# A fused two-block transformer on one core: the head norm of the delta layer taken into the output projection, wider norm sums, modulation sums out of the first weight slab, and a mask and a weight part moved in each pair of dilated heads

## The reference

```python
def _gated_deltanet(qkv, gate, ...):
    ...
    q = (_l2norm(q) * (DN_HEAD_K ** -0.5))
    k = _l2norm(k)
    ...
    o = o * lax.rsqrt(jnp.mean(o * o, axis=-1, keepdims=True) + EPS) * g_out   # the head norm, 4 heads of 128
    o = o * jax.nn.silu(gate)

def first_block(x, mem, ...):
    ...
    mix = jnp.concatenate([attn_o, dn_o], axis=-1) @ w_out        # features 0-511 attention, 512-1023 delta layer
    x = x + _rms_norm(mix, g_mix_post)
    c = _memory_cross_attention(_rms_norm(x, g_cross_pre), _rms_norm(mem, g_mem), w_cq, w_ckv, w_co)
    x = x + _rms_norm(c, g_cross_post)
    f = _swiglu(_rms_norm(x, g_ffn_pre), w_gate_up, w_down)
    x = x + _rms_norm(f, g_ffn_post)

def second_block(x, c, ...):
    mod = (silu(c) @ w_ada + b_ada)                               # shift, scale, gate of each part
    h = h + 0.5 * gt * swiglu(modulate(rms_norm(h, norm_g), sh, sc), ffn_w_in, ffn_w_out)
    ...
def dilated_mixer(u, ...):
    # 3 groups: q, k = rope(rms_norm(.)), banded attention, softmax over the groups
```

## Time and profile before

| | |
|---|---|
| three runs, us | 3774.03, 3776.29, 3779.77 (median 3776.29) |
| profiled execution, us | 3775.3 |
| its span, us | 3773.5 |
| mean granted clock of PE | 0.976 |
| PE busy, share of the span | 3598.0 us, 95% |
| DVE busy | 1940.0 us, 51% |
| ACT busy | 1436.7 us, 38% |
| product matmuls L848, L853, L854 on x | 2936 each |

### The profile page before, as it was taken

The page is one execution under the profiler, slowest core; times in us unless marked ns, Lnnn a source line. Parts: engine busy times, 40 slices in busy tenths (PEclk is TensorE's granted clock), DMA queues, the critical chain, the costliest instruction groups (busy, mean ns, idle before and its releaser), DMA issues.

```text
span 3773.5 us, 49208 instructions
## 1 busy us (share of the span) xinstructions
PE 3598.0 (95%) x18880; PEld 2897.3 (77%) x18880; DVE 1940.0 (51%) x3906; ACT 1436.7 (38%) x2555; POOL 107.7 (3%) x183
## 2 busy tenths in 40 slices
PE   7989999999999999999999989999899998889999
PEld 6879976878887888766666668888788886678887
DVE  6767665565565545555555554334433345764333
ACT  3342132422232222555665643223322234863222
POOL 0000001011001000000000000000000000000000
PEclk9999999999998999999999989999899999999999
DMA  5200046145544554211111212222222220012222
GB/s 212 95 1 1 1 156 245 67 139 189 176 165 141 178 184 134 70 65 51 51 68 51 79 54 89 89 103 91 76 100 101 73 92 29 2 46 89 90 92 76
DMA packets 47156, 359.74 MB, mean 95 GB/s; under 512 B 5216, under 2 KB 5600, under 8 KB 28128
## 3 DMA queue, kind: packets, MB, share of 16 engines
q1 hardware_dynamic: 23472, 269.35, 19.6%
q0 software_dynamic: 23472, 87.50, 6.9%
HBM read 354.73 MB, written 2.10 MB: 95 GB/s over the span
## 4 chain that ended last, share of the span: by engine, by line
PE 84%; DVE 7%; issue 3%; ACT 3%; DVEq 1%; DMA 1%; ACTq 0%; PEld 0%; PEldq 0%; POOL 0%; SPq 0%; POOLq 0%
PE bank L848 22%; PE bank L854 22%; PE bank L853 21%; PE bank L1775 5%; PE bank L2093 1%; PE bank L2081 1%; PE bank L2591 1%; DVE w_lo_sb L1285 1%; PE bank L2558 1%; PE bank L989 1%; PE bank L2069 1%; PE bank L828 1%; PE bank L810 1%; PE bank L2580 1%; PE bank L2108 1%
## 5 line engine op out<-in xcount | busy, mean ns | idle before, releaser
L848 PE MATMUL bank<-x_hi_sb,w_hi_sb 128*128 128x512 f32 x2936 | 1177.4, 401 | 54.9 <-DVE w_lo_sb L1285 16.3
L854 PE MATMUL bank<-x_hi_sb,w_lo_sb 128*128 128x512 f32 x2936 | 1152.1, 392 | 0.0
L853 PE MATMUL bank<-x_lo_sb,w_hi_sb 128*128 128x512 f32 x2936 | 1151.3, 392 | 0.0
L848 PEld LDWEIGHTS bank<-x_hi_sb,w_hi_sb 128*128 128x128 f32 x2936 | 555.4, 189 | 226.1 <-issue 82.0
L1108 ACT ACTIVATE w_hi_sb<-slab_sb 128x1024 fp32r<-128x1024 f32 (+2 forms) x555 | 508.4, 937 | 511.0 <-PE bank L848 317.5
L1285 DVE TENSOR_TENSOR w_lo_sb<-slab_sb,w_hi_sb 128x1024 fp32r<-128x1024 f32 (+2 forms) x555 | 581.7, 1078 | 199.5 <-ACT w_hi_sb L1108 185.7
L854 PEld LDWEIGHTS bank<-x_hi_sb,w_lo_sb 128*128 128x128 f32 x2936 | 555.2, 189 | 120.1
L853 PEld LDWEIGHTS bank<-x_lo_sb,w_hi_sb 128*128 128x128 f32 x2936 | 556.4, 190 | 110.0 <-issue 0.5
L1451 DVE TENSOR_TENSOR hid_sb<-silu_gate_sb,bank 128x512 f32<-128x512 f32 x110 | 75.6, 687 | 600.3 <-PE bank L854 600.3
L848 PE MATMUL bank<-hid_hi_sb,w_hi_sb 128*128 128x512 f32 x880 | 342.8, 390 | 0.0
L854 PE MATMUL bank<-hid_hi_sb,w_lo_sb 128*128 128x512 f32 x880 | 342.6, 389 | 0.0
(11 more groups left out here) (368 smaller groups left out, 3696.5 us busy)
## 6 DMA issues: line engine op xcount, KB each, us to landing
slab_sb<-weights SPq DMA_DIRECT2D x79, 2048.0 KB, 7.9
keep_sb<-ada POOLq DMA_DIRECT2D x137, 512.0 KB, 4.5
slab_sb<-weights SPq DMA_DIRECT2D x44, 1536.0 KB, 6.5
slab_sb<-weights SPq DMA_DIRECT2D x20, 1280.0 KB, 6.0
tables_sb<-ada POOLq DMA_DIRECT2D x12, 512.0 KB, 6.0
work_sb<-ada POOLq DMA_DIRECT2D x11, 512.0 KB, 5.6
h_sb<-x SPq DMA_DIRECT2D x4, 512.0 KB, 7.6
out<-h_sb SPq DMA_DIRECT2D x8, 256.0 KB, 2.1
```

The lines of the kernel that those rows point to most:

```text
L848: mm = pe.matmul(out, w_hi[p][:, w], hi, start=first, stop=False)
L853: pe.matmul(out, w_hi[p][:, w], lo, start=False, stop=False)
L854: return pe.matmul(out, w_lo[p][:, w], hi, start=False, stop=last)
```

## The change

Six edits in one:

- Stage "delta_out" is gone. `pe_delta_out` sums the four heads' squares (32 columns of ones in place of one), runs 8 fillers, and begins the first slab of w_out with k-tiles 0 to 3 (attention, which needs no head norm) of its four output tiles, with the head norm's spreads after the first and second of them, two heads each, into the two banks of the scores ring; then k-tiles 4 to 7 of the four tiles. ACT squares head by head, DVE scales and gates each head between weight parts. `mem` is loaded after "delta", and the next modulation rows after the heads are done.
- The norm sums are 128 columns wide (`P`), and 42 (`WIDE`) where three sums share a bank. The count of matmuls stays.
- The window's 32 sums become 8 matmuls with 512 columns and weights 64 wide (`one_slots`, two per step into the two halves of a bank), a copy by ACT (`rows_summed`) and four transposes, and everything after them that `pe_delta_ahead` does comes one step earlier. The 12 decay sums become 3 with more columns.
- No modulation sum stands in a "first" step; "mid" and "last" get them.
- In each dilated pair the first two instructions of mask(1) go ahead of weigh(0), and `w_lo_part(7)` ahead of `rope(1, 0)` (on ACT `w_hi_part(7)` ahead of `swap_in(1, 0)`).
- 9 fillers stand ahead of `stage_end("ffn_down")`; `OUT_SEAT` 1 becomes 0 (which bank is used); a semaphore is gone.

```diff
-OUT_SEAT = 1
+OUT_SEAT = 0
+WIDE = 42
...
+        def sums_in(bank, n, wide):
+
+            return bank[:, n * NB * wide:(n + 1) * NB * wide].rearrange("p (b w) -> p b w", w=wide)
+
-        def pe_sums_of(e, n, tile):
+        def pe_sums_of(e, n, tile, stop=False):
 
             for b in range(NB):
-                at = n * NB + b
-                e.eng.matmul(e.S.bank[e.sums][:, at:at + 1], tile[:, b * P:(b + 1) * P], ones1, start=at == 0, stop=False)
+                mm = e.eng.matmul(sums_in(e.S.bank[e.sums], n, e.wide)[:, b, :], tile[:, b * P:(b + 1) * P],
+                                  K("ones")[:, 0:e.wide], start=n == b == 0, stop=stop and b == NB - 1)
+            return mm
 
         def pe_sums_open(e, cross=None, first=False):
 
             pe = e.eng
-            e.sums = e.give(e.S, e.sc)
+            e.sums, e.wide = e.give(e.S, e.sc), P if cross is None else WIDE
...
-            if i < 2:
-                if i == 0:
-                    e.norms = e.give(e.A, e.acc)
-                for j in DN_TILES[4 * i:4 * i + 4]:
...
-                    for b in range(NB):
-                        at = j * NB + b
-                        mm = pe.matmul(e.A.bank[e.norms][:, at:at + 1], sq[:, j, b * P:(b + 1) * P], ones1, start=True,
-                                       stop=True)
...
+            if i == 0:
+                s = e.give(e.A, e.acc)
+                for n in range(4):
+                    pe.wait_ge(squared, e.nth(squared))
+                    pe.wait_ge(queries_squared, n + 1)
+                    for x in range(2):
+                        mm = pe.matmul(e.A.bank[s][HALF * x:HALF * x + HALF, :], K("one_slots")[:, 3 - n:67 - n],
+                                       sq[:, 4 * x + n, :], start=n == 0, stop=n == 3)
+                mm.then_inc(e.A.full[s], 1)
+            if i == 1:
+                pe.wait_ge(rows_summed, 1)
+                t = e.give(tp, e.tp)
+                for b in range(NB):
+                    mm = pe.transpose(turn_bank[t][:, b * P:(b + 1) * P], sq[:, 0, b * P:(b + 1) * P], ident)
+                mm.then_inc(tp.full[t], 1)
...
             e.stage_end("delta")
-            pe_stay_busy(e, 10)
-            pe_cols(e, f_t, 4, NB, False, 1, 6)
-            for j in range(4):
-                pe_spread(e, NB, 1, j)
-            e.stage_end("delta_out")
...
+        def pe_delta_out(e):
...
+            pe_stay_busy(e, 8)
+            e.slab.next()
+            ps, seats = [], []
+            for t in range(PARTS):
+                ps.append(e.take(part, e.part))
+                seats.append(e.give(e.A, e.acc))
+                for kt in range(DH):
+                    if t == 0:
+                        pe.wait_ge(x_lo_ready, e.nth(x_lo_ready))
+                    pe_product(e, seats[t], ps[t], slice(kt * P, (kt + 1) * P), x_hi[:, kt, :], x_lo[:, kt, :], kt == 0, False)
+                if t == 0:
+                    pe.wait_ge(inverted, e.nth(inverted))
+                if t < 2:
+                    spread(2 * t)
+                    spread(2 * t + 1)
+            for t in range(PARTS):
+                for kt in range(DH, KT):
+                    if t == 0:
+                        pe.wait_ge(x_lo_ready, e.nth(x_lo_ready))
...
+            for j in range(DH):
+                s = e.take(e.S, e.sc)
+                e.link(dve.scalar_tensor_tensor(out=y[:, DH + j, :], in0=y[:, DH + j, :], scalar=V("g_dn_out"),
+                                                in1=e.S.bank[s][:, :], op0=ALU.mult, op1=ALU.mult), dve_step)
+                tt(y[:, DH + j, :], y[:, DH + j, :], b1_gate[:, j, :], ALU.mult).then_inc(scaled, 1)
+                dve.drain().then_inc(e.S.free[s], 1)
+                if j < 2:
+                    dve_w_lo(e, 2 + j, D)
+            dve.drain().then_inc(normed, 1)
+            for k in range(DH, KT):
+                low(k)
...
             out_tile(0)
+            mask(1, 0)
             weigh(0)
             out_tile(1)
-            mask(1)
+            mask(1, 1)
...
             mask(3)
+            w_lo_part(7)
             rope(1, 0)
-            w_lo_part(7)
...
             def modulations(half, at):
-                if at in ("first", "mid", "last"):
-                    dve_ada(e, 2 if at == "mid" else 3)
-                elif half == 0:
+                if at in ("mid", "last"):
+                    dve_ada(e, 3 - half)
+                elif at != "first" and half == 0:
                     dve_ada(e, 1)
...
-            if stage_over("delta_out"):
+            if stage_over("delta"):
                 eng.dma_start(mem_in, a["mem"]).then_inc(mem_loaded, 16)
+                eng.wait_ge(normed, KT + DH + 1)
                 load_ada(1)
```

More of the change, by code:

```diff
@@ L1020, in pe_sums_close @@
                 for b in range(NB):
-                    at = n * NB + b
-                    mm = pe.matmul(e.S.bank[e.sums][:, at:at + 1], tile[:, b * P:(b + 1) * P], ones1,
-                                   start=False, stop=at == len(tiles) * NB - 1)
+                    mm = pe.matmul(sums_in(e.S.bank[e.sums], n, e.wide)[:, b, :], tile[:, b * P:(b + 1) * P],
+                                   K("ones")[:, 0:e.wide], start=False, stop=n == len(tiles) - 1 and b == NB - 1)
             mm.then_inc(e.S.full[e.sums], 1)
@@ L1060, in act_root @@
             s = e.take(ring, seat)
-            act.activation(root[:, 0:cols], ring.bank[s][:, 0:cols], ACT.Sqrt, scale=scale,
+            sums = ring.bank[s][:, 0:cols * wide].rearrange("p (b w) -> p b w", w=wide)[:, :, 0]
+            act.activation(root[:, 0:cols], sums, ACT.Sqrt, scale=scale,
                            bias=small[:, 120:121]).then_inc(rooted, 1)
@@ L1713, in act_delta_ahead @@
             act = e.eng
-            if i == 2:
-                act_root(e, 32, 1.0)
+            if i == 0:
+                s = e.take(e.A, e.acc)
+                act.activation(sq[:, 0, :], e.A.bank[s][:, :], ACT.Copy).then_inc(rows_summed, 1)
+                act.drain().then_inc(e.A.free[s], 1)
+            if i == 1:
+                t = e.take(tp, e.tp)
+                act.activation(root[:, 0:32].rearrange("p (x n b) -> p b x n", x=2, n=4),
+                               turn_bank[t][:, :].rearrange("p (b x c) -> p b x c", b=NB, x=2)[:, :, :, 0:4], ACT.Sqrt,
+                               bias=small[:, 120:121]).then_inc(rooted, 1)
+                act.drain().then_inc(tp.free[t], 1)
                 act_table(e, ACT.Exp)
@@ L2369, in take_scores, with mask, roots, mask_first @@
                 return s
-            def mask(u):
+            def mask(u, half=None):
                 if not attending:
                     return
+                if half != 1:
+                    mask_first(u)
+                if half != 0:
+                    mask_others(u)
+            def roots(u):
+                return [[d_inv[old][:, 6 * u + 2 * g + hh:6 * u + 2 * g + hh + 1] for hh in range(2)] for g in range(3)]
+            def mask_first(u):
                 if u == 3:
@@ L2956, in out_tile @@
                 act_copy_square(e, k, f_t[:, k, :])
-            act_linear_parts(e, y, 1, out_tile, first=4, ahead=0)
+            for k in range(KT):
+                out_tile(k)
+                if k < PARTS:
+                    act_w_hi(e, k, D)
             e.stage_end("w_out")
@@ L3235, in out_tile @@
                     dve_ada(e, 2)
-            dve_linear_parts(e, y, 1, out_tile, first=4, ahead=0)
+            for k in range(KT):
+                out_tile(k)
+                if k < PARTS:
+                    dve_w_lo(e, k, D)
             e.stage_end("w_out")
@@ L3274, in later_modulations @@
             def later_modulations(half, at):
-                if at in ("first", "mid", "last"):
-                    dve_ada(e, 2)
-                elif half == 0 or at == 0:
+                if at in ("mid", "last"):
+                    dve_ada(e, 2 if at == "mid" else 3)
+                elif at != "first" and (half == 0 or at == 0):
                     dve_ada(e, 1)
```

111 lines of the change are left out of this document (68 added, 43 removed).

## The result

The changed kernel takes 3722.19 us (median of 4 runs, 3718.33 to 3724.34) against 3777.15 for the kernel before: a ratio of 0.9855, 95% interval 0.9839 to 0.987. 3725 was forecast. The profiled execution took 3722.46, its span 3720.7.

What follows compares the result with a forecast made beforehand. PE bounds the kernel (84% of the span), losing time standing still or at half clock. Gains 13.3 + 11.5 + 8.4 + 10 + 8 = 51.2 from 3775.3 give 3724, plus 1.0 for the median: 3725 us, range 3709 to 3746.

Steps and rivals of the forecast that it cites:

- A: Head norm in w_out: attention products start before the head norm, tile 3 done at 500.2; gain 13.3 us, from 9.5 to 15.
- D: Dilated pairs: PE's waits for w_lo (6.6 us) and mask (5.2 us) go; gain 10 us, from 4 to 12.
- 32 sums at 0.117 are 3.7, 16 fillers 1.9: Ahead of w_out's first product: sums and fillers from 469.1 us at 0.117 us each, so products start at 474.7.
- B: Norm sums: wider columns cost nothing and keep the clock at full where narrow sums ran at half; 11.5 us, 0 to 20.
- 6.7 and half of 9.9: Wide norm sums: 6.7 us from 1524.2 and later stretches; 9.9 us at 746 and 1131.7, halved for having only 42 columns.
- C: First steps of two FFNs: without modulation sums, waits shrink 3.1 and 1.9 us, half clock returns 1.7 each; 8.4, 5 to 9.
- I give 1.8 back: Dilated pairs: new waits on weigh and rope take back a quarter of a microsecond in each of seven pairs.
- E: Window stage: 16 instructions of 512 columns replace two groups of 32 sums, fewer decay sums; gain 8 us, from 4 to 11.
- The clock rival: Norm and window sums: clock falls regardless of width, wide sums gain 0, window part 4.8; 3740 us, chance 0.17.
- The dilated waits did not move: Rival, dilated stage: PE waits for weigh(0) or rope instead, gain there 0 to 2 us; 3733 to 3735, chance 0.10.
- w_out did not stall behind DVE: Rival, w_out: DVE's scalings run 6 us late, PE waits some 3 us ahead of k-tile 4; 3730 us, chance 0.08.
- wait for a modulation row: Rival, fourteen pairs taking three rows: POOL's refill takes about 18 us, PE waits in each; 3776 or more, chance 0.03.

## Why the prediction held, step by step

The time came 3 us below the forecast, inside the range. That it came so near is luck: A is below its low bound, D above its high one, and the two errors cancel.

- **A** (13.3, at least 9.5): 8.2. The mechanism of the overlap was right: attention half first, spreads between, the scalings beside the products, and mem hidden, with no wait where I feared one (the spread of head 3 or k-tile 4). The failed step is "32 sums at 0.117 are 3.7, 16 fillers 1.9": I took the full clock of before for granted, though the change removed the ten fillers that stood ahead of the sums, where PE then stood still 2.07 us. The half clock cost 5.0; fillers in that place gave back 3.5.
- **B** (11.5; its terms, 6.7 and half of 9.9, make 11.65): 9.8 in the profiled pair, 8.7 by medians and 8.3 by products on taking it back. It is a little oversized, and its reason held only in part. I wrote that the wide sums rest on the clock falling "during narrow ones", and counted the fillers as a cost to be hidden. Between the FFNs the fillers do the larger part: all of 4.2 in the changed kernel, and in the kernel before as much as the width alone, 3.5 and 3.6. Width works behind w_ckv: in all nine traces with wide sums the lead grows by 1.5 to 1.6 there, and in none with narrow ones. At the end of the second FFN it gives 0.8, in seven of the nine. The failed step is "the clock fell during narrow ones. This is what the wide sums rest on": 42-wide sums went at half too, for 10.2 us behind w_co. My half for 42 columns was the right caution for a wrong reason: behind w_co they gave nothing in the changed kernel and 4.6 in the run with wide sums alone.
- **C** (8.4): 8.0, both waits and both falls of the clock as stated; the ten pairs with three sums show no wait. That the clock falls behind the second, shorter wait is not sure: it did not when the sums were put back.
- **D** (10, at most 12): 18.3. The step that failed is "I give 1.8 back" and, under it, taking the idle time of the earlier trace rows as the price, over a window that ends ahead of the last round. Nothing was given back, and the two moves are worth 7.7 and 7.2 by products. A wait shown as 0.83 costs more, as PE's timeline in the kernel before shows (start, duration, idle before):

```profile
1640.50 0.40 PE L854 MATMUL bank<-x_hi_sb,w_lo_sb 128*128 128x512 f32 x1
1641.73 0.50 PE L848 MATMUL bank<-x_hi_sb,w_hi_sb 128*128 128x512 f32 x1 [0.83 <-DVE w_lo_sb L1285]
1642.07 0.39 PE L853 MATMUL bank<-x_lo_sb,w_hi_sb 128*128 128x512 f32 x1
```

  Products otherwise start 0.23 apart. Here the steps are 1.23 and 0.34: 1.0 and 0.11 lost, 1.1 for an idle time of 0.83, since that is counted from the modelled end of a pipelined product. Seven such waits went, not the eight of the earlier trace rows: 7.7. The seven for the mask, 0.75 on average, cost 0.83 each: 5.8. The last round, whose mask waits fell from 7.4 to 5.4 us, gave 2.2. A fall of the clock at 1930 that did not recur gave 1.6, and the remaining 1.0 is spread in small steps. 18.3 is a high reading: in the seven other traces with both moves the step is 15.2 to 17.4, and the four with the order of before differ by 3.4 among themselves.
- **E** (8): 9.1 in the pair, 10.3 for the part alone by products (10.8 by medians), so somewhat undersized. The overlap of the two halves of a bank held; that the half clock around the sums goes too was in no term.
- **The rivals.** The clock rival came true in the single place behind w_co and, unforeseen, at the head sums. The dilated waits did not move; w_out did not stall behind DVE; in none of these kernels does PE wait for a modulation row in the FFNs.

## What to carry to other kernels

Price a wait by the distance of the starts around it, not by the idle time printed beside it: here that was a third more for the products and a tenth more for the mask's waits. Before taking fillers away or putting short sums behind a stage end, look whether PE stands still ahead of them; here a gap of 2.07 us was followed by sums and fillers that took 5.0 us longer, and 2.25 us of fillers in it gave back 3.5. And where one kernel's runs differ by 5 to 10 us, compare the starts of the same product in two traces, stage by stage.

## What the runs showed of the hardware

- The same 24 sums of 42 columns behind w_co ran at half clock in the changed kernel (5.19 us for the second group of 24) and inside a window of 1.00 in the run with wide sums alone, with the same instructions from the first group's start to the first product behind; the programs ahead of that differ. So the granted clock of such a stretch is not a property of its code alone. Executions of one program differ too: of the window part alone, one had a mean granted clock of 0.981 and took 3757.03 us, another 0.977 and 3771.04. The Trainium skill, TensorE: Matmul & The Clock Gate, Part 1, calls the warm-up at a kernel's start run-variable. These stretches lie in the middle of a kernel, so they do not test that.
- Narrow float32 matmuls cost as much as wide ones up to 128 columns: at full clock 32 spreads of 128 columns take 3.74 us, 32 sums of 32 columns 3.66 in the run with fillers ahead of the head sums, 16 sums of 42 columns 1.96 in the changed kernel and 16 of one column 1.93 in the run with narrow sums.
- Two matmuls with 64-wide weights into the two halves of a bank overlap when the loop alternates them: 16 with 512 columns take 3.65 us at full clock (4.75 and 5.35 where half clock fell into them), where 0.43 each, the distance of 512-column float32 matmuls with 128-wide weights in the kernel before, would be 6.9.
